# Seven half-width block products for projection tiles 36 to 45 of a hybrid decoder's mixer, with one weight sum written into the weight slab

## What is computed

```python
h = rms_norm(x, mix_norm[l])                       # 288 tokens x 1024 features
proj = h @ w_in                                    # 1024 x (2048 | 1536+8 | 2304 | 3072)
...                                                # HGRN2 recurrence of the first 2048 columns (4 heads)
...                                                # Mamba-2 SSD of the next 1544
att = proj[..., OFF_ATT:OFF_GATE].reshape(b, L, 3, 3, 4, 64)   # 3 groups of q, k, v
qg = rms_norm(att[:, :, g, 0], q_norm[g]); kg = rms_norm(att[:, :, g, 1], k_norm[g]); vg = att[:, :, g, 2]
gates = sigmoid(proj[..., OFF_GATE:])
out = (gates[:, :, 0] * (y_hg @ w_out_hg) + gates[:, :, 1] * (y_ssm @ w_out_ssm)
       + gates[:, :, 2] * (y_att @ w_out_att)) @ w_o
```

## Time and profile before

| | us |
|---|---|
| median of 3 runs | 2094.76 |
| lowest and highest | 2093.45, 2094.96 |
| the profiled execution, its own time | 2095.35 |
| its span in the profile | 2093.6 |

### The profile page before, as it was taken

How to read it: one execution, slowest core, us unless ns; L and a number is a source line. 1 busy time by engine, 2 the same in 40 slices (tenths; PEclk the granted TensorE clock), 3 DMA queues, 4 the chain that set the end, 5 groups by cost and what they waited for, 6 DMA issues and landing times.

```text
span 2093.6 us, 45799 instructions
## 1 busy us (share of the span) xinstructions
PE 2061.1 (98%) x20277; PEld 1372.8 (66%) x20277; DVE 784.8 (37%) x1493; ACT 404.9 (19%) x772; POOL 157.2 (8%) x222
## 2 busy tenths in 40 slices
PE   7999999999999999999999999999999999999998
PEld 5977777778999997777777735353544444444435
DVE  5896333535676578643254310100101010101013
ACT  3423424311221143333342210000000000000000
POOL 3501020000000031112100010000000000000001
PEclk9999999999999999999999999999999999999999
DMA  5434535695554543453477699999999999999996
GB/s 167 142 110 142 172 115 161 191 269 158 147 157 147 159 141 122 128 161 116 151 198 221 257 381 412 409 411 409 412 408 412 407 411 408 403 411 395 413 411 239
DMA packets 287993, 548.81 MB, mean 262 GB/s; under 512 B 12883, under 2 KB 218501, under 8 KB 271348
## 3 DMA queue, kind: packets, MB, share of 16 engines
q1 hardware_dynamic: 279808, 535.85, 70.9%
q10 hardware_dynamic: 6644, 5.58, 0.9%
q0 software_dynamic: 1344, 4.45, 0.6%
HBM read 527.15 MB, written 22.50 MB: 263 GB/s over the span
## 4 chain that ended last, share of the span: by engine, by line
PE 93%; DMA 3%; DVE 2%; POOL 1%; issue 1%; ACT 1%; POOLq 0%; DVEq 0%; ACTq 0%
PE bank L1080 90%; PE bank L1086 3%; DMA mem<-in_w_moe_up_dram 1%; DMA mem<-in_w_moe_down_dram 1%; ACT mem L2057 1%; DVE mem L2543 0%; DVE mem L2880 0%; DVE mem L2547 0%; DVE hflat L2576 0%; POOL quarterm L937 0%; DVE mem L2906 0%; POOL lmask L913 0%; POOL lmask L915 0%; DVE col L2913 0%; DVE hflat L2543 0%
## 5 line engine op out<-in xcount | busy, mean ns | idle before, releaser
L1080 PE MATMUL bank<-mem 128*32 128x256 f32 (+9 forms) x13288 | 1097.9, 387 | 11.9 <-DVE mem L2880 3.5
L1080 PEld LDWEIGHTS bank<-mem 128*32 128x32 f32 (+3 forms) x13288 | 713.6, 128 | 377.6 <-issue 219.6
L1080 PE MATMUL bank<-hflat,mem 128*128 128x288 f32 (+3 forms) x2688 | 572.9, 371 | 0.9 <-ACT hflat L2057 0.7
L1080 PEld LDWEIGHTS bank<-hflat,mem 128*128 128x128 f32 (+2 forms) x2688 | 443.2, 188 | 102.9 <-issue 12.2
L2057 ACT ACTIVATE mem<-bank 128x288 f32<-128x288 f32 (+10 forms) x423 | 180.1, 430 | 818.0 <-PE bank L1080 753.5
L1080 PE MATMUL bank<-mem,steps 128*32 128x384 f32 (+1 forms) x3072 | 289.8, 539 | 0.0
L2543 DVE TENSOR_TENSOR mem<-mem 128x512 f32<-128x512 f32 (+10 forms) x328 | 231.2, 733 | 29.3 <-PE bank L1080 19.1
L1080 PEld LDWEIGHTS bank<-mem,steps 128*32 128x32 f32 x3072 | 102.5, 110 | 184.0 <-issue 181.9
L2547 DVE SCALAR_TENSOR_TENSOR hflat<-hflat,bank 128x512 f32<-128x512 f32 x24 | 15.1, 683 | 411.6 <-ACT hflat L2057 411.6
L2057 ACT ACTIVATE hflat<-bank 128x512 f32<-128x512 f32 (+1 forms) x40 | 19.6, 554 | 571.1 <-PE bank L1080 548.7
L2057 ACT ACTIVATE mem<-mem 128x1152 f32<-128x1152 f32 (+9 forms) x125 | 92.1, 738 | 99.2 <-DVE mem L2635 63.9
(11 more groups left out here) (250 smaller groups left out, 747.2 us busy)
## 6 DMA issues: line engine op xcount, KB each, us to landing
mem<-in_w_moe_up_dram SPq DMA_DIRECT2D x64, 2048.0 KB, 22.6
mem<-in_w_moe_down_dram SPq DMA_DIRECT2D x56, 2048.0 KB, 23.1
mem<-in_w_moe_up_dram SPq DMA_DIRECT2D x32, 2304.0 KB, 24.7
mem<-in_w_in_dram SPq DMA_DIRECT2D x70, 1024.0 KB, 5.4
mem<-in_w_moe_up_dram SPq DMA_DIRECT2D x16, 1536.0 KB
mem<-in_w_ffn_up_dram SPq DMA_DIRECT2D x44, 512.0 KB, 5.1
mem<-in_cache_kv_w_dram SPq DMA_DIRECT2D x26, 512.0 KB, 4.7
mem<-in_cache_kv_w_dram SPq DMA_DIRECT2D x74, 128.0 KB, 4.6
```

Of the source, the lines that this page charges most:

```text
L1080: return mm(out, lhsT, rhs, start=start, stop=stop, skip_group_check=True)
```

## The change

Pairs 18 to 22 (tiles 36 to 45: keys and values of attention group 1, queries, keys and values of group 2) join `SEVEN`. So there are five more pairs in each of the two layers. Beside it:

- One of the four weight sums, a21 + a22, is written over block a21 in the slab, so that a pair needs three buffers of sums instead of four; there are six sets of three (`SUMS_IN` says which pair uses which). The order of the four sums is now s3, s1, s2, s4, and PE waits for the second before its fourth product.
- The pieces of the new pairs go to `parts_late`, one of which lies over G and one over zexp and the later `spread_x`.
- VectorE makes the new sums behind `qe` (18), `z_gated` (19), the fifth operation of `dt_sums` (20), `hgrn_head(0)` (21) and `hgrn_head(1)` (22). The copy into `spread_x` leaves `conv_silu` for `hgrn_norm_out`, and PE's `ssd_x_rows` waits for `hg_done` in place of the second `vexp_ready`.
- GpSimd joins pair 18 ahead of the first `s0_scaled`, pair 19 ahead of the second, pair 20 behind it, pair 21 behind the third and pair 22 behind the fourth.
- `st_hg` moves to another place, for room.

```diff
-SEVEN = (4, 5, 6, 7, 8, 9)
+SEVEN = (4, 5, 6, 7, 8, 9, 18, 19, 20, 21, 22)
+SUMS_IN = (0, 1, 2, 0, 1, 2, 3, 4, 5, 4, 5)
...
-        msum = [view(over, 0, 4, KT // 2, P), view(over, 2048, 4, KT // 2, P), view(arena, 15872, 4, KT // 2, P)]
-        parts = [view(over, 42 * T + 7 * TH * i, 7, TH) for i in range(2)]
+        msum = [view(over, at0, 3, KT // 2, P) for at0 in (0, 1536, 3072, 6 * T, 18 * T, 18 * T + 1536)]
+        parts_early = [view(over, 42 * T + 7 * TH * i, 7, TH) for i in range(2)]
+        parts_late = [view(arena, A0_, 7, TH) for A0_ in (4 * T + 8 * PADT, 14720 + 8 * PADT)]
...
-                for p in SEVEN:
-                    s = parts[SEVEN.index(p) % 2]
+                def join_pair(p):
+
+                    s, dst = parts_of(p), pair_out(p)
                     pool.wait_ge(*drained(("piece", L, p, 2)))
                     step(gp.tensor_tensor(s[:, 4], s[:, 4], s[:, 0], ALU.add))
                     step(gp.tensor_tensor(s[:, 5], s[:, 5], s[:, 4], ALU.add))
...
+                for p in range(4, 10):
+                    join_pair(p)
+
...
                 for h in range(HH):
+                    if h < 2:
+                        join_pair(18 + h)
                     pool.wait_ge(*at("hg_tail", L))
                     pool.wait_ge(*filled(("hg_x", L, h)))
...
                         "s0_scaled", L, h + 1)
+                    if h > 0:
+                        join_pair(19 + h)
...
-                (a11, a12), (_, a22) = quarters(slab(n_slab[0], KT, 2 * P))
+                (a11, a12), (s1, a22) = quarters(slab(n_slab[0], KT, 2 * P))
...
-                pe.wait_ge(*at("vexp_ready", L, 2))
+                pe.wait_ge(*at("hg_done", L))
...
+                if p == 19 and t % 2 == 0:
+                    act.wait_ge(*at("z_gated", L))
...
-                four_sums([msum[i % 3][:, j] for j in range(4)], a11, a12, a21, a22, lambda k: mixer_sums(L, p, k))
+                s2, s3, s4 = sums_of(p)
+                tt(s3, a11, a21, ALU.subtract).then_inc(sums_done, 1)
+                dve.wait_ge(*mixer_sums(L, p, 1))
+                tt(a21, a21, a22, ALU.add).then_inc(sums_done, 1)
+                dve.wait_ge(*mixer_sums(L, p, 2))
+                tt(s2, a21, a11, ALU.subtract).then_inc(sums_done, 1)
+                dve.wait_ge(*mixer_sums(L, p, 3))
+                tt(s4, a12, s2, ALU.subtract).then_inc(sums_done, 1)
+                dve.wait_ge(*mixer_sums(L, p, 4))
...
             def hgrn_norm_out(L):
+                dve.wait_ge(*pair_joined(L, 22))
+                step(ve.tensor_copy(fourfold(spread_x), tail_of(xs[:, 0:6, :])))
...
                 say(tt(qe, hgp[:, 0:4, TP:T], taild.rearrange("p h b i -> p h (b i)"), ALU.mult), "qe_ready", L)
+                mixer_weight_sums(L, 18)
...
+                dve.wait_ge(*at("kd_ready", L))
+                mixer_weight_sums(L, 19)
                 dt_sums(L)
                 hgrn_head(L, 0)
+                mixer_weight_sums(L, 21)
                 conv_silu(L)
                 values_by_sequence(L, 1)
                 hgrn_head(L, 1)
+                mixer_weight_sums(L, 22)
                 qk_normed(L, 0)
```

More of the change, by code:

```diff
@@ L167, in hybrid_decoder @@
         qe = view(arena, 18392, HH, TS)
-        st_hg = view(arena, A0, HH, P)
+        st_hg = view(small, 512, HH, P)
         o_hg, osq, o_rstd = dist, view(arena, A1, HH, T), view(arena, A1 + 1664, HH, T)
@@ L547, in pair_joined, with parts_of, sums_of, pair_out @@
             return joined, len(SEVEN) * L + SEVEN.index(p) + 1
+        def parts_of(p):
+            return (parts_early if p < 10 else parts_late)[SEVEN.index(p) % 2]
+        def sums_of(p):
+            return [msum[SUMS_IN[SEVEN.index(p)]][:, j] for j in range(3)]
+        def pair_out(p):
+            a = heads_of((2 * p - 28) // 6, (2 * p - 28) % 6, 1)[0] if p >= 14 else 0
+            v = hgp[:, 2 * p:2 * p + 2, :] if p < 8 else zT[:, 2 * p - 16:2 * p - 14, :] if p < 10 else att[:, a:a + 2, :]
+            return v.rearrange("p m (j t) -> p m j t", j=2)
         def quarters(w):
@@ L607, in plan_slabs @@
             for s in range(NS_AG):
-                add_slab(("proj", L, 29 + 2 * s), (0, rows_of(w_in[L], 0, KT, OFF_ATT + 256 * s, 256)))
+                add_slab(("piece", L, 14 + s, 2) if 14 + s in SEVEN else ("proj", L, 29 + 2 * s), (0, rows_of(w_in[L], 0, KT, OFF_ATT + 256 * s, 256)))
             for br, w in enumerate((w_out_hgrn, w_out_ssm)):
@@ L1134, in proj_pair @@
                     take_slab(KT, 2 * P)
-                (a11, a12), (_, a22) = quarters(slab(n_slab[0], KT, 2 * P))
+                (a11, a12), (s1, a22) = quarters(slab(n_slab[0], KT, 2 * P))
                 t1, t2, t3, t4 = (tok_m[:, j] for j in range(4))
-                s1, s2, s3, s4 = (msum[SEVEN.index(p) % 3][:, j] for j in range(4))
+                s2, s3, s4 = sums_of(p)
                 third = lambda acc, i: acc[:, TH * i:TH * i + TH]
@@ L1142, in proj_pair @@
                     product(third(a, 1), a12, hT[:, h:KT, 0:TH], False)
-                    pe.wait_ge(*mixer_sums(L, p, 1))
+                    if p == SEVEN[0]:
+                        pe.wait_ge(*mixer_sums(L, p, 1))
                     close_bank(product(third(a, 2), a22, t4, False), ("piece", L, p, 0))
-                    product(third(open_bank(("piece", L, p, 1)), 0), s1, t1, True)
+                    b = open_bank(("piece", L, p, 1))
+                    pe.wait_ge(*mixer_sums(L, p, 2))
+                    product(third(b, 0), s1, t1, True)
                     return
                 b = psum(("piece", L, p, 1))
-                pe.wait_ge(*mixer_sums(L, p, 2))
+                pe.wait_ge(*mixer_sums(L, p, 3))
                 product(third(b, 1), s2, t2, False)
-                pe.wait_ge(*mixer_sums(L, p, 3))
                 close_bank(product(third(b, 2), s3, t3, False), ("piece", L, p, 1))
@@ L2259, in keep_pieces @@
                 i = SEVEN.index(p)
-                out = halve_out if p >= 6 else copy_out
+                out = halve_out if 6 <= p < 10 else copy_out
+                if p == 19 and t % 2 == 0:
+                    act.wait_ge(*at("z_gated", L))
                 if t % 2 == 0 and i >= 2:
@@ L2264, in keep_pieces @@
                     key, n = ("piece", L, p, piece), 1 if piece == 2 else 3
-                    out(parts[i % 2][:, 3 * piece:3 * piece + n, :].rearrange("p j t -> p (j t)"), key,
+                    out(parts_of(p)[:, 3 * piece:3 * piece + n, :].rearrange("p j t -> p (j t)"), key,
                         psum(key)[:, 0:n * TH])
@@ L2584, in mixer_weight_sums @@
                 dve.wait_ge(slab_in[n % RING], 16 * slab_dmas[n])
-                if i >= 3:
-                    dve.wait_ge(*filled(("piece", L, SEVEN[i - 3], 2)))
+                earlier = [SEVEN[j] for j in range(i) if SUMS_IN[j] == SUMS_IN[i]]
+                if earlier:
+                    dve.wait_ge(*filled(("piece", L, earlier[-1], 2)))
                 (a11, a12), (a21, a22) = quarters(slab(n, KT, 2 * P))
-                four_sums([msum[i % 3][:, j] for j in range(4)], a11, a12, a21, a22, lambda k: mixer_sums(L, p, k))
+                s2, s3, s4 = sums_of(p)
+                tt(s3, a11, a21, ALU.subtract).then_inc(sums_done, 1)
[6 more added lines that the diff above has]
+                dve.wait_ge(*mixer_sums(L, p, 4))
             def hgrn_inputs(L):
@@ L2740, in conv_silu @@
                         say(ins, "xs_ready", L)
-                step(ve.tensor_copy(fourfold(spread_x), tail_of(xs[:, 0:6, :])))
             u, dt_tmp, cum, wl = (dts[0:SH, i, :] for i in (0, 1, 2, 4))
```

20 lines of the change are left out of this document (9 added, 11 removed).

## The result

The changed kernel takes 2101.19 us (median of 8 runs, 2099.84 to 2103.31), the kernel before 2094.72 (8 runs, 2093.45 to 2096.43). The ratio is 1.0029, 95% interval 1.0020 to 1.0038: 6.5 us slower. The forecast was 2101.6. Two executions out of all that are reported here ran at a mean granted clock of 0.95, one of the kernel before (2167.72 us) and one of an experiment (2162.26), and are left out of every number.

What follows compares the result with a forecast made beforehand. TensorE (PE) was taken as the bound, with VectorE just in time at heads 1 and 2 and becoming the bound after the change. Layers 3.6 and 3.25 later give +6.9 on 2095.35, moved by 0.59 to 2101.6 us; range 2091.5 to 2105.5.

Steps and rivals of the forecast that it cites:

- The saving of a pair: On PE, a pair in seven products takes 6.86 us against 7.96, saving 1.10; ten pairs 11.0 without waits.
- Up to head 0: Pairs 18 and 19 gain 2.20 us ahead of head 0's state products; sums of 18 to 20 cost nothing.
- The chain to head 1: VectorE's work from head 0's last addition to head 1's `hg_x` copy grows from 7.34 to 9.40 us, plus 2.0 for joining.
- The joining of pair 20: GpSimd's additions slow VectorE's small operations on the chain to head 1 by 2.0 us, bounds 0 and 3.4.
- The forecast sign: In the profile after, several small operations of `conv_silu` beside GpSimd's joining take 0.5 us or more.
- The wait: PE idles about 5 us ahead of head 1's `own_row` products in both layers, released by VectorE's copy.
- The clock: Behind the wait at head 1 PE's clock halves, costing 1.9 us in each layer, bounds 0 to 3.4.
- my worst rival: Joinings cost their full length and the clock falls twice in a layer, at head 2 too: 2110 us; chance 0.07.
- The sum: Layers end 3.6 and 3.25 us later, together +6.9, giving 2101.6 us, +0.33%; chance 0.50.
- Joinings miss: GpSimd's joinings don't lengthen VectorE's chains: 2091.9 us, or 2095.7 with the clock still falling; chance 0.17.
- full saving: PE never waits and all 11.0 us are saved: 2083.8 us; chance 0.08.
- The clock holds: No half clock behind the wait at head 1, so both layers lose the 1.9 us cost: 2097.8 us; chance 0.18.

Runs made afterwards that it cites:

- the kernel with three late pairs: Changed kernel with pairs 20 and 21 made as ordinary tiles again, their sums and joinings dropped: 2092.43 us, ratio 0.9996.
- the last kernel: Changed kernel, joinings 20 and 21 held back, pair 21's sums behind head 1's copy and `hgrn_head(1)`, `values_by_sequence(2)` and head 2's copy ahead of `qk_normed`: 2084.92 us.
- the filled kernel: Changed kernel with useless products on PE, 15 ahead of head 1's `own_row` products and 4 ahead of head 2's: 2104.89 us, on another chip 2101.82.

## Why the prediction was right

**The mechanism held.** The forecast wait at head 1 is there in both layers, released by the copy, and so are the wait at head 2 and the half clock. The kernel before with only the load of the sums shows that the chain alone does it; the removal of the sums from the chain shows the reverse.

**The saving of a pair** was put too high. Pair 18 took 177.54 - 173.53 = 4.01 and 181.16 - 178.11 = 3.05, so 7.06 and not 6.86: it saves 0.90 us, not 1.10. The two pieces of the earlier trace rows ran on into products of the same kind, these hand over to others. That is the likely reason; no run separates it. Head 0 stands 192.60 - 173.53 = 19.07 behind the start of tile 36 against 20.71: 1.64 gained in place of 2.20. In the kernel with three late pairs, which has no wait ahead of head 0, it is 1.80, two pairs at 0.90. Ten pairs are worth 9.0; the last kernel is 9.5 below before, the same within its interval.

**Up to head 0 the prediction had luck.** It put the sums of pairs 18 to 20 at nothing, because `dt_ready` ended more than 5 us ahead of its use and was the last thing that VectorE owed PE there. It was not: behind it comes the copy for head 0, with a margin of 3.45. And `dt_ready` itself ended at 191.33 in place of 187.59, its last operation taking 2.05 in place of 0.45 beside the scaling of head 0's state. The margin was used up to the last tenth. Another microsecond of VectorE's work there would have been a wait in each layer, as the sums of pair 20 behind `dt_ready` showed.

**The chain to head 1** came to 11.0 us, forecast 9.40 + 2.0 = 11.4. Its terms were off in opposite directions. The sums took 3.36 with their gap in place of 2.65: 2.87 us even alone (a row at 210.58), where the earlier trace rows had 2.62, and 0.46 more beside the end of the joining of pair 19, which I had not placed there. The operations are as long as before, 0.69; in the new order each waits for the one ahead of it, while in the old one the third and the fourth did not, and started 0.61 instead of 0.73 behind their predecessors. The joining of pair 20 cost 1.0 and not 2.0.

By the Trainium skill, "SBUF — State Buffer", section "Who interferes with whom", the port pair that VectorE and GpSimd share is an exclusive lock, and a VectorE instruction with two SBUF inputs contends with a GpSimd instruction that reads SBUF. The estimate that the joining would therefore cost its full 3.07 us is not borne out: it cost 1.0. The lock itself the trace does not contradict: three of the small operations took longer (0.36, 0.36 and 0.67), and each ended within 0.05 us of the end of a GpSimd addition. Between them four others passed at 0.19. So each of the first four additions held up one operation, the last of them `values_by_sequence(1)`, for 0.17 to 0.47 us, which adds up to the 1.0. The nine operations of `conv_silu` have a median of 193 ns without the joining and 364 beside it, and the joining itself took 3.66 us in place of 3.37. The forecast sign, several operations of 0.5 or more, came only in part: beside the joining there was one in layer 0 and there were two in layer 1.

**The wait** was 4.09 and 4.25, forecast about 5, since PE arrived later in its own work than I had it (10.1 us behind head 0 in place of 9.8) and the chain was shorter. Head 1 is 1.65 late in layer 0 (1.86 forecast; 1.90 and 1.51 in layer 1), counted from the start of tile 36.

**The clock** cost 1.6 us a fall (6.8 in place of 5.2 up to `pairs`), forecast 1.9 for one in each layer. There were three falls in the profiled run, so 4.9 in place of 3.8: the second one in layer 0 is what my worst rival had for both layers. Without them the stretch is the 56.2 us of the filled kernel, 3.0 longer than before; less the 1.64 gained ahead, each layer would be only 1.4 late. The clock is more than half of the loss.

**The sum.** Layer 0 ended 4.5 us later (forecast 3.6), layer 1 3.25 (3.25), 7.8 in place of 6.9. The rest of the program, where nothing on PE is edited, gave back 2 us in this one profile, so its span is only 5.7 longer; over 8 runs the difference is 6.5. Of that agreement to half a microsecond a part is luck: saving and joining too high, sums and number of falls too low.

**The rivals.** "Joinings miss" is refuted by the 1.0 us that the joining cost the chain, "full saving" by the waits. "The clock holds", 2097.8, did not happen here, but was not far off: with a wait of 3.10 it held in one layer of two.

## What to carry to other kernels

When work is moved from the bounding engine to one with a low busy share, read the helper's chain between two points where the bounding engine needs it, in us: here a margin of 0.06 us decided, not 37% busy. Do it for every such point, and for the last thing owed at each: at head 0 a margin of 3.45 us vanished unseen. Place the new work in a gap of the helper that is bounded by a third engine (the 2.87 us ahead of `dt_ready`), or behind the release that the bounding engine waits for. And count a wait on TensorE twice, once for itself and once for the clock behind it.

## What the runs showed of the hardware

- Behind waits of 2.4 to 4.3 us of PE at head 1, between stretches in which it had no idle time, the granted clock fell to half in 7 of 8 cases, six times for 3.41 us and once for 6.8; behind the two waits of 2.93 at head 0 it fell too, once for 3.41 and once for 6.8. It began as late as some 2 us behind the wait's end, and twice ahead of it. Each of 3.41 us at head 1 cost 1.6 to 1.7 us. Behind the 1.35 us at head 2 it fell in 2 of 6, behind waits of up to 1.25 us at head 1 in none of 12. The same wait of 3.10 us did it in one layer and not in the other, so the length of the wait alone does not decide it.
- Falls also began where these kernels have no such wait, at 441 to 449, at 1133 and at 1194 to 1211 us, each in some of the 14 traces and not in the others.
- The mean granted clock of a run lay at 0.994 to 0.997 for the changed kernel, at 0.996 to 1.000 for the one before, and at 0.998 to 1.000 for the fastest one.
- Stages without any edit differ between profiles by some us: the part behind the second stretch took 1148 to 1152 us in all traces but one (1155, with half clock for 6.8 and 3.4 us in it). A gain of 2 us that one profile shows elsewhere is no gain.
